# Hierarchical router of a mixture of experts: five blocks of logits in one pass, and the rows of slot numbers made ahead of the dispatch

## What is computed

```python
pg = jax.nn.softmax((t @ wg + bg), axis=-1)            # 4 groups
g = jnp.argmax(pg, axis=-1)
p_top = jnp.take_along_axis(pg, g[:, None], axis=-1)
le = (t @ we + be).reshape(ntok, N_GROUPS, EXPERTS_PER_GROUP)   # 4 x 4
le_g = jnp.take_along_axis(le, g[:, None, None], axis=1)[:, 0]
v, idx = lax.top_k(jax.nn.softmax(le_g, axis=-1), 2)
w_k = p_top * v / jnp.sum(v, axis=-1, keepdims=True)
comb = sum over the two of one_hot(g * 4 + idx, 16) * w_k
out = sum over experts of ((silu(t @ w_gate) * (t @ w_up)) * comb) @ w_down   # inner width 512
```

## Time and profile before

| | us |
|---|---|
| median of 3 runs (lowest, highest) | 486.19 (484.97, 486.24) |
| profiled execution | 485.3 |
| its span, first to last instruction | 483.2 |
| busy in the span: PE | 446.0 (92%) |
| DVE | 238.6 (49%) |
| ACT | 121.5 (25%) |
| POOL | 63.0 (13%) |

### The profile page before, as it was taken

One profiled execution on the slowest core, in us unless ns is written; L12 is line 12 of the kernel. 1 busy time (PEld: TensorE's weight loads), 2 busy tenths in 40 slices (PEclk: granted clock), 3 DMA queues, 4 the chain that ended last, 5 costly groups with the idle time before them and its releaser, 6 DMA issues.

```text
span 483.2 us, 6512 instructions
## 1 busy us (share of the span) xinstructions
PE 446.0 (92%) x2394; PEld 239.7 (50%) x2394; DVE 238.6 (49%) x448; ACT 121.5 (25%) x242; POOL 63.0 (13%) x61
## 2 busy tenths in 40 slices
PE   2678999999999999799999999999999999998882
PEld 1244555556654456595554454455554444553420
DVE  3552713848743347951124153454445545536767
ACT  2400168682230225352111110111111111121200
POOL 2000024356550421021000000000000000000300
PEclk9989999999999999999999999999999999998988
DMA  8999996855999026801999899999999999997003
GB/s 231 383 387 387 288 387 236 305 217 187 323 378 366 15 84 265 320 30 33 363 387 420 366 340 393 390 431 427 425 419 420 425 429 423 416 429 301 1 2 130
DMA packets 32611, 146.90 MB, mean 304 GB/s; under 512 B 3688, under 2 KB 4520, under 8 KB 24376
## 3 DMA queue, kind: packets, MB, share of 16 engines
q1 hardware_dynamic: 31376, 143.40, 76.3%
q10 hardware_dynamic: 1032, 2.81, 1.5%
q0 software_dynamic: 160, 0.10, 0.3%
HBM read 144.72 MB, written 1.58 MB: 303 GB/s over the span
## 4 chain that ended last, share of the span: by engine, by line
PE 75%; SPq 11%; DVE 6%; issue 3%; ACT 2%; DMA 1%; POOLq 1%; POOL 0%; DVEq 0%; ACTq 0%
PE PS L1805 19%; PE PS L1845 11%; PE PS L1671 9%; PE PS L1569 8%; PE PS L1812 6%; SPq L420 5%; PE PS L1875 5%; PE PS L1746 4%; SPq L425 3%; PE PS L1497 2%; PE PS L1546 2%; PE PS L1852 1%; PE PS L1603 1%; PE PS L1882 1%; PE PS L1827 1%
## 5 line engine op out<-in xcount | busy, mean ns | idle before, releaser
L1805 PE MATMUL PS<-ring,xs 128*64 128x256 f32 x896 | 102.9, 382 | 0.0
L1805 PEld LDWEIGHTS PS<-ring,xs 128*64 128x64 f32 x896 | 61.8, 137 | 36.8 <-issue 8.3
L1569 PE MATMUL PS<-hT,ring 128*128 128x388 f32 x192 | 67.5, 502 | 2.6 <-DVE hT L902 2.6
L1227 DVE SCALAR_TENSOR_TENSOR y<-PS,comb,y 128x1024 f32<-128x1024 f32 x42 | 53.5, 1277 | 0.3 <-PE PS L1882 0.3
L1845 PE MATMUL PS<-ring,hTs 128*64 128x512 f32 x224 | 52.9, 616 | 0.0
L1569 PEld LDWEIGHTS PS<-hT,ring 128*128 128x128 f32 x192 | 36.7, 194 | 31.6 <-issue 8.3
L1176 DVE SCALAR_TENSOR_TENSOR hid<-sg,PS 128x256 f32<-128x256 f32 x18 | 10.7, 612 | 46.8 <-PE PS L1805 36.0
L1458 POOL TENSOR_TENSOR y<-y,g2r 128x1024 f32<-128x1024 f32 x1 | 2.4, 2373 | 234.4 <-DVE y L1227 234.4
L1845 PEld LDWEIGHTS PS<-ring,hTs 128*64 128x64 f32 x224 | 15.3, 141 | 31.3 <-issue 31.2
L738 ACT CAST yh<-PS 128x512 fp32r<-128x512 f32 x13 | 7.6, 585 | 89.0 <-PE PS L1845 55.1
L1214 DVE TENSOR_TENSOR yl<-PS,yh 128x512 fp32r<-128x512 f32 x13 | 9.0, 692 | 41.9 <-ACT yh L738 41.9
(11 more groups left out here) (272 smaller groups left out, 601.6 us busy)
## 6 DMA issues: line engine op xcount, KB each, us to landing
ring<-in_ex_w_gate SPq DMA_DIRECT2D x16, 2048.0 KB, 12.0
ring<-in_ex_w_up SPq DMA_DIRECT2D x16, 2048.0 KB, 14.0
ring<-in_ex_w_down SPq DMA_DIRECT2D x16, 2048.0 KB, 12.7
ring<-in_w_ada SPq DMA_DIRECT2D x11, 2048.0 KB, 11.9
ring<-in_w_in SPq DMA_DIRECT2D x2, 2048.0 KB, 23.2
ring<-in_w_out SPq DMA_DIRECT2D x2, 2048.0 KB, 10.3
ring<-in_w_ada SPq DMA_DIRECT2D x2, 1024.0 KB, 14.9
ring<-in_w_in SPq DMA_DIRECT2D x2, 1024.0 KB, 14.7
```

Source lines behind the costliest of these rows:

```text
L1227: dve.scalar_tensor_tensor(out=y, in0=src, scalar=comb[:, i, e:e + 1], in1=y, op0=ALU.mult, op1=ALU.add).then_inc(s["acc_done"], 1)
L1569: mm = pe.matmul(PS[:, w % 4, 0:W], wt[:, k, (w % 4) * P:(w % 4 + 1) * P], hT[:, k, :], start=(k == 0), stop=(k == KD - 1))
L1805: mm = pe.matmul(PS[HALF * h:HALF * (h + 1), bank, 0:FE // 2], x(k, HALF), w[:, k, h * (FE // 2):(h + 1) * (FE // 2)], start=(k == 0), sto ...
```

## The change

The expert and group logits go through `first_max` together, as five blocks of four values in each token tile. The second pass stays. The sum of both marks is multiplied by the winning group once, in float32 and in bfloat16, ahead of the scan; the two single marks are multiplied by it behind L1085, ahead of `low_part(1)`, and VectorE waits for these before it multiplies the ranks. On TensorE the twelve matmuls of the rows of slot numbers, with their waits for the slot numbers (`pw_done`) and for ScalarE's copy to mrow (`mrow_sb` 5), move ahead of the first four banks of the dispatch. Tiles of the later weight steps get other names and places, with the same sizes. The diff's core:

```diff
+        oh5 = at("oh5", router0, [P, NT, NG + NE])
+        mark5 = at("mark5", router0 + 256, [P, NT, NG + NE])
+        top5 = at("top5", router0 + 512, [P, 2, NT, 5])
...
-            first_max(gl, C_COD4, og, rs[:, 0, :], rt[:, 5, :, 0:NG], rs[:, 11, :])
-            x4, oh14, oh24, tmp4 = by_group(rt[:, 7]), by_group(oh1), by_group(oh2), by_group(rt[:, 4])
-            first_max(by_group(el), C_COD4, oh14, mx1, tmp4, top)
-            link(dve.scalar_tensor_tensor(out=rt[:, 7], in0=oh1, scalar=-2e30, in1=el, op0=ALU.mult, op1=ALU.add))
-            first_max(x4, C_COD4, oh24, mx2, tmp4, top)
+            mx5 = top5[:, 0]
+            first_max(by_group(lg[:, :, :]), C_COD4, by_group(oh5[:, :, :]), mx5, by_group(mark5[:, :, :]), top5[:, 1])
+            mx0, mx1 = mx5[:, :, 0], mx5[:, :, 1:]
+            og, first = oh5[:, :, 0:NG], oh5[:, :, NG:]
+            oh1, oh2, pair, asg = rt[:, 4], rt[:, 5], rt[:, 6], marks16[:, :, :]
+            mx2, top = rs[:, 0:4, :].rearrange("p a i -> p i a"), rs[:, 4:8, :].rearrange("p a i -> p i a")
+            link(dve.scalar_tensor_tensor(out=rt[:, 7], in0=first, scalar=-2e30, in1=el, op0=ALU.mult, op1=ALU.add))
+            first_max(by_group(rt[:, 7]), C_COD4, by_group(oh2), mx2, by_group(rt[:, 4]), top)
             og4 = og.unsqueeze(3).broadcast_to([P, NT, NG, EPG])
-            step(dve.tensor_tensor(oh14, oh14, og4, ALU.mult))
-            link(dve.tensor_tensor(oh24, oh24, og4, ALU.mult))
-            dve.tensor_tensor(asg, oh1, oh2, ALU.add).then_inc(s["assign_done"], 1)
-            link(dve.tensor_tensor(rt[:, 4], oh1, oh2, ALU.add))
+            link(dve.tensor_tensor(pair, first, oh2, ALU.add))
+            dve.tensor_tensor(by_group(asg), by_group(pair), og4, ALU.mult).then_inc(s["assign_done"], 1)
+            link(dve.tensor_tensor(by_group(pair), by_group(pair), og4, ALU.mult))
...
+            dve.tensor_tensor(before16[:, :, :], rt[:, 7], pair, ALU.subtract).then_inc(s["assign_done"], 1)
+            step(dve.tensor_tensor(by_group(oh1), by_group(first), og4, ALU.mult))
+            step(dve.tensor_tensor(by_group(oh2), by_group(oh2), og4, ALU.mult))
             low_part(1)
             dve.wait_ge(s["rank_ps"], 1)
+            dve.wait_ge(s["dve_step"], n_step[0])
             step(dve.tensor_tensor(rt[:, 7], place_ps, oh1, ALU.mult))
...
-            pe.wait_ge(s["h2lo"], 2)
-            pe.wait_ge(s["x1_done"], NT)
-            for i in range(NT):
-                for n in range(4):
-                    dispatch(n, (i,))
             pe.wait_ge(s["pw_done"], 1)
             pe.wait_ge(s["mrow_sb"], 5)
             for q in range(2):
...
             mm.then_inc(s["prow_ps"], 1)
+            pe.wait_ge(s["h2lo"], 2)
+            pe.wait_ge(s["x1_done"], NT)
+            for i in range(NT):
+                for n in range(4):
+                    dispatch(n, (i,))
```

More of the change, by code:

```diff
@@ L678, in _ @@
                     act.wait_ge(s["gap_done"], 1)
-                    act.activation(rt[:, 6, :, 0:NG], rt[:, 5, :, 0:NG], ACT.Exp).then_inc(s["pos_pool"], 1)
-                    act.activation(rs[:, 5, :], rs[:, 4, :], ACT.Exp).then_inc(s["pos_pool"], 1)
+                    act.activation(mark5[:, :, 2 * NG:3 * NG], mark5[:, :, NG:2 * NG], ACT.Exp).then_inc(s["pos_pool"], 1)
+                    act.activation(rs[:, 9, :], rs[:, 8, :], ACT.Exp).then_inc(s["pos_pool"], 1)
             act.wait_ge(s["route_done"], 1)
@@ L1068, in by_group @@
                 return v.rearrange("p i (g e) -> p i g e", e=EPG)
-            og, oh1, oh2, asg = rt[:, 0, :, 0:NG], rt[:, 1], rt[:, 2], marks16[:, :, :]
-            mx1, mx2, top = rt[:, 3, :, 0:NG], rt[:, 3, :, NG:2 * NG], rt[:, 3, :, 2 * NG:3 * NG]
-            first_max(gl, C_COD4, og, rs[:, 0, :], rt[:, 5, :, 0:NG], rs[:, 11, :])
-            x4, oh14, oh24, tmp4 = by_group(rt[:, 7]), by_group(oh1), by_group(oh2), by_group(rt[:, 4])
-            first_max(by_group(el), C_COD4, oh14, mx1, tmp4, top)
@@ L1080, in _ @@
-            dve.tensor_tensor(asg, oh1, oh2, ALU.add).then_inc(s["assign_done"], 1)
-            link(dve.tensor_tensor(rt[:, 4], oh1, oh2, ALU.add))
+            link(dve.tensor_tensor(pair, first, oh2, ALU.add))
+            dve.tensor_tensor(by_group(asg), by_group(pair), og4, ALU.mult).then_inc(s["assign_done"], 1)
+            link(dve.tensor_tensor(by_group(pair), by_group(pair), og4, ALU.mult))
             link(dve.tensor_tensor_scan(rt[:, 7].rearrange("p i e -> p (i e)"), cst[:, C_SEG:C_SEG + NT * NE],
-                                        rt[:, 4].rearrange("p i e -> p (i e)"), 0.0, ALU.mult, ALU.add))
@@ L1085, in _ @@
-            dve.tensor_tensor(before16[:, :, :], rt[:, 7], rt[:, 4], ALU.subtract).then_inc(s["assign_done"], 1)
+                                        pair.rearrange("p i e -> p (i e)"), 0.0, ALU.mult, ALU.add))
+            dve.tensor_tensor(before16[:, :, :], rt[:, 7], pair, ALU.subtract).then_inc(s["assign_done"], 1)
+            step(dve.tensor_tensor(by_group(oh1), by_group(first), og4, ALU.mult))
+            step(dve.tensor_tensor(by_group(oh2), by_group(oh2), og4, ALU.mult))
             low_part(1)
@@ L1090, in _ @@
             place_ps = PS[:, 0, 0:NT * NE].rearrange("p (i e) -> p i e", e=NE)
+            dve.wait_ge(s["dve_step"], n_step[0])
             step(dve.tensor_tensor(rt[:, 7], place_ps, oh1, ALU.mult))
-            step(dve.tensor_tensor(rt[:, 4], place_ps, oh2, ALU.mult))
+            step(dve.tensor_tensor(rt[:, 6], place_ps, oh2, ALU.mult))
             step(dve.tensor_copy(totoff[:, :, :], PS[:, 0, NT * NE:(NT + 2) * NE].rearrange("p (a e) -> p a e", e=NE)))
@@ L1095, in _ @@
             step(dve.tensor_reduce(pw[:, 0, :], rt[:, 7], AX.X, ALU.add))
-            step(dve.tensor_reduce(pw[:, 1, :], rt[:, 4], AX.X, ALU.add))
+            step(dve.tensor_reduce(pw[:, 1, :], rt[:, 6], AX.X, ALU.add))
             dve.wait_ge(s["dve_step"], n_step[0])
@@ L1140, in _ @@
                 dve.tensor_scalar(io[:, q, :], io[:, q, :], -1.0, None, ALU.add).then_inc(s["io_done"], 1)
[L1142 to L1145, removed]
+            gaps, over, gap = mark5[:, :, 0:NG], mark5[:, :, NG:2 * NG], rs[:, 8, :]
+            step(dve.tensor_tensor(over, gl, wide(mx0, NG), ALU.subtract))
+            link(dve.tensor_tensor(gaps, mx2, mx1, ALU.subtract))
+            link(dve.tensor_tensor(gaps, gaps, og, ALU.mult))
+            link(dve.tensor_reduce(gap, gaps, AX.X, ALU.add))
             dve.nop().then_inc(s["gap_done"], 1)
@@ L1150, in _ @@
             dve.wait_ge(s["pos_pool"], 2)
[L1151 to L1158, removed]
+            total, ratio = rs[:, 10, :], rs[:, 9, :]
+            link(dve.tensor_reduce(total, mark5[:, :, 2 * NG:3 * NG], AX.X, ALU.add))
+            link(dve.tensor_scalar(rs[:, 11, :], ratio, 1.0, None, ALU.add))
+            link(dve.tensor_tensor(total, total, rs[:, 11, :], ALU.mult))
+            link(dve.reciprocal(wk[:, 0, :], total))
+            link(dve.tensor_tensor(wk[:, 1, :], wk[:, 0, :], ratio, ALU.mult))
+            step(dve.tensor_tensor(rt[:, 6], oh1, wide(wk[:, 0, :], NE), ALU.mult))
+            link(dve.tensor_tensor(rt[:, 7], oh2, wide(wk[:, 1, :], NE), ALU.mult))
+            dve.tensor_tensor(comb[:, :, :], rt[:, 6], rt[:, 7], ALU.add).then_inc(s["comb_done"], 1)
             counts = {}
```

## The result

The changed kernel takes 480.89 us in the median of 20 runs (479.12 to 487.05), the kernel before 485.71 in the median of 20 beside it (482.63 to 487.77). The ratio is 0.9915, with a 95% interval of 0.9892 to 0.9937: 4.1 us less (3.1 to 5.2). (The medians are 4.8 apart. The ratio agrees with that of the means, 481.1 to 485.3, from which the changed kernel's one slow execution, 487.05, is left out.) Forecast were 2.0 less, 484.2 in a range of 482.5 to 485.9. The profiled execution took 480.1, with a span of 478.0; both are 5.2 under those of before.

What follows compares the result with a forecast made beforehand. TensorE's matmuls were taken to bound the kernel, waiting on VectorE's routing string. The dispatch going on 1.94 us earlier plus 0.08 without a pipe refill made 2.02, taken as 2.0: 486.19 becomes 484.2, range 482.5 to 485.9.

Steps and rivals of the forecast that it cites:

- The path: From the router's logits to the first expert matmul: 2.02 us earlier, taken as 2.0 saved at the end.
- Pass: VectorE's routing: one pass over 60 values replaces the group's and first expert pass, 1.28 us, 0.94 saved.
- marks: VectorE ahead of the scan: three small instructions instead of four, 0.13 saved; L1085 starts 1.07 earlier in all.
- multiplications: VectorE between L1085 and L1031: two multiplications by the group, not waited for, 0.25 us lost.
- the copy to mrow as what comes last: ScalarE's copy, over at 198.78, is the last thing the rows of slot numbers need; they start at 198.87.
- the stall gone: TensorE's dispatch: the 0.20 us wait for the third tile of sel goes.
- ScalarE's copies in time: Emptying the dispatch's banks: first copy over by 204.1, TensorE asking at 204.37, 0.25 us of room.
- no load late: Expert stage: the tightest load found keeps 2.8 us of room; rival that loads absorb the gain, chance 0.02.
- The clock's term: TensorE's granted clock over rows and dispatch: stayed full in the profile, so no term in the 2.02 us sum.
- the rival: TensorE's clock, rows and dispatch: one fall more costs 1.7 us, 485.9, chance 0.13; two or more, chance 0.05.
- without the fall within 440 to 445: Rival, TensorE's clock in that late stretch: one fall fewer gives 482.5 us, chance 0.12.

Runs made afterwards that it cites:

- pass alone: The changed kernel with the twelve row matmuls put back behind the dispatch's first banks: 482.21 us, ratio 0.9948 to the kernel before.
- filled kernels: Kernel before, five-block pass only, moved row matmuls only, and both, each with unread matmuls in TensorE's idle stretches, routing and tail: 481.92, 481.13, 481.27, 480.72 us.
- before again: The kernel before, run again with no edit: 484.43 us in the median of 12, ratio 0.9993.
- rows alone: The kernel before with only the twelve row matmuls moved ahead of the dispatch, routing as before: 484.22 us, ratio 0.9978.
- before, both stretches filled: The kernel before plus unread matmuls in TensorE's idle time, eleven ahead of the wait for the marks, ten ahead of the dispatch: 483.23 us, ratio 0.9952.
- before, second stretch filled: The kernel before plus only the ten unread matmuls ahead of the dispatch: 484.18 us, ratio 0.9965.
- changed again: The changed kernel, run again with no edit: 480.55 us, ratio 0.9920 to the kernel before.
- filling the tail: Unread matmuls in four idle stretches of the last two experts; added to the changed kernel: 480.41 us, ratio 0.9893 to the kernel before.

## Why the prediction was right in its sign and wrong in its size

**The path was right.** Pass, marks, multiplications, the copy to mrow as what comes last, the stall gone, ScalarE's copies in time, no load late: each step came within 0.2 of its number, and 1.91 of the 2.02 arrived at the first expert matmul. Of the missing 0.11, 0.08 is the length of the rows of slot numbers (1.33, not 1.25), which now start behind 0.80 of idle time; that this is the reason was not tested.

**The clock's term failed: the sum had it at nothing.** The prediction read "It stayed full in 196 to 201, although TensorE was busy for only 2.16 of those 5 us" from one execution, and took the stretch for harmless. It is not: two of the three profiles of unfilled kernels that keep the full idle stretch ahead of the dispatch show a fall there, at a price of 2.58 and, for the pass alone, 28.02 - 26.76 = 1.26. In the rival, falls "can come or go", one more or one fewer, each with a small chance of its own, as if the change had no part in them. "Against it: the idle time shrinks (1.39 to 0.3, 1.45 to 0.75)" stood there as an argument and got no price. The price should have been a term of the sum: what the kernel before loses on average to falls in its routing. Measured, filling the stretches gains 2.3 us (1.1 to 3.5) in the kernel before, and nothing that can be told in the changed one. 1.9 of path and 2.3 of clock make 4.2; measured were 4.1 (3.1 to 5.2). That the clock is the second half is shown by the filled kernels, which are 1.8 apart on the path and lose what scatter they had. That all of the 2.3 are falls over the dispatch is not shown, as the next part says.

**The tail.** The rival "without the fall within 440 to 445" was counted as one event at 1.7. The profiled pair shows two falls gone, 3.4 in all. All profiles with an unfilled tail, from the ranks on and as long as TensorE has work (the starts of the falls are read from windows of 0.1 us):

| profile | addition to expert 0 | expert 0 to end | falls start at |
|---|---|---|---|
| before | 27.61 | 263.3 | 441.4, 458.4 |
| before again | 30.19 | 261.5 | 199.8, 459.2 |
| pass alone | 28.02 | 263.2 | 199.2, 441.6, 458.6 |
| rows alone | 26.75 | 263.3 | 441.3, 458.3 |
| before, both stretches filled | 27.60 | 261.5 | 440.8 |
| before, second stretch filled | 27.60 | 263.6 | 441.0, 458.1 |
| changed | 25.70 | 259.9 | none |
| changed again | 25.70 | 259.9 | none |

Falls of the tail come at the same two places, within half a microsecond of the start of sixteen matmuls (in the first profile at 441.08) and of four later ones. These four stand behind 1.17 us of idle time, which every kernel has; here in the kernel before, before again, before with both stretches filled, and changed:

```profile
458.20 3.55 PE L1917 MATMUL PS<-y,cst 128*128 128x512 f32 x4 [1.17 <-POOL y L1459]
...
459.05 3.63 PE L1917 MATMUL PS<-y,cst 128*128 128x512 f32 x4 [1.16 <-POOL y L1459]
...
458.05 1.98 PE L1927 MATMUL PS<-y,cst 128*128 128x512 f32 x4 [1.16 <-POOL y L1459]
...
454.65 1.98 PE L1924 MATMUL PS<-y,cst 128*128 128x512 f32 x4 [1.17 <-POOL y L1466]
```

So the profiles have one fall or two in the tail of each kernel but the changed one, and none in either profile of that. Against a cause in the change speaks what filling the tail gains on average: in the kernel before 483.23 to 481.92, about 1.3 (two sessions, on different chips), or 0.9 by the ratios to the kernel beside (0.9952 to 0.9933); in the changed kernel 0.1 to 0.5 by the medians, or 1.1 by the ratios (0.9915 to 0.9893). These are equal within their intervals. Whether the changed kernel's tail is hit less often by more than chance, and whether filling the routing spares the tail as well, was not settled.

**The rest.** The Trainium skill ("TensorE: Matmul & The Clock Gate", Part 1) was drawn on for a watch on activity that does not start with the kernel, by which falls would move from run to run. The trace agrees: there is a fall at the dispatch in one of two profiles of the same kernel. What stood before it were idle stretches of 1.39 and 1.44, with little work between them. The loads never came near the path, and the copy to mrow moved as it should.

Not tried: a count of how many executions of the kernel before fall at the dispatch (there is one profile for each run, and of the other executions only the mean clock), and idle time put back into the changed kernel.

## What to carry to other kernels

Short idle stretches of TensorE ahead of a dense one can cost twice: their own length, and now and then half the clock over what follows; a change that closes them can earn more than its instructions, and one profile in which the clock held is no proof. Look at several executions, and before you price such a change, fill the stretches of the kernel before with matmuls that nobody reads: what that gains is the clock's part, and what is left between filled kernels is the path's, with a scatter of about 1 us in place of 3 to 5. For chains of small VectorE instructions, count links: 0.20 us for 12 values a partition and 0.25 for 60, so that merging two passes is worth nearly one of them, and an instruction that nobody waits for costs half.

## What the runs showed of the hardware that was not expected

The granted clock fell over the dispatch though TensorE was not idle for more than 1.5 us at a time in the 15 us before, and stayed at half for nearly 7 us with TensorE busy on the dispatch behind it (0.50 over 200 to 205, 0.83 over 205 to 210). Twenty-one matmuls of bfloat16 in otherwise idle time, 2.6 us of work added, made the kernel 2.3 us faster. And most of the scatter of this kernel's times, 5 us from the fastest to the slowest of 20, goes with this clock: filled in the routing and the tail, 6 executions of the same kernel stay within 1.1.
